# Where a delta layer's scan loads its decay row and makes its exponent arguments

## The reference, cut to what matters

```python
diff = gcum[..., :, None] - gcum[..., None, :]
decay_incl = jnp.where(incl, jnp.exp(jnp.where(incl, diff, 0.0)), 0.0)
a_mat = jnp.einsum('nbhid,nbhjd->nbhij', k_beta, kc) * decay_strict
t_mat = unit_lower_inverse(a_mat, cb)
...
def step(state, inp):
    q_i, k_i, w_i, u_i, qk_i, g_i = inp
    v_new = u_i - jnp.einsum('bhck,bhkv->bhcv', w_i, state)
    o_i = (jnp.einsum('bhck,bhkv->bhcv', q_i * jnp.exp(g_i)[..., None], state)
           + jnp.einsum('bhcj,bhjv->bhcv', qk_i, v_new))
    g_last = g_i[..., -1:]
    k_dec = k_i * jnp.exp(g_last - g_i)[..., None]
    state = state * jnp.exp(g_last)[..., None] + jnp.einsum('bhck,bhcv->bhkv', k_dec, v_new)
    return state, o_i
```

## Time and profile before

| what | value |
|---|---|
| median of three executions | 1416.29 us (1416.02 to 1417.29) |
| profiled execution, its own time | 1415.07 us |
| its span, first to last instruction | 1413.3 us |
| TensorE matmul busy | 1364.9 us, 97% of the span |
| VectorE busy | 822.2 us, 58% |
| ScalarE busy | 439.0 us, 31% |
| GpSimd busy | 269.5 us, 19% |
| mean granted TensorE clock | 0.999 of full speed |
| one head of the delta layer | 88.5 to 91.0 us |

### The profile page before, as it was taken

How to read it: one execution, slowest core, us unless ns; L and a number is a source line. 1 busy time by engine, 2 the same in 40 slices (tenths; PEclk the granted TensorE clock), 3 DMA queues, 4 the chain that set the end, 5 groups by cost and what they waited for, 6 DMA issues and landing times.

```text
span 1413.3 us, 30732 instructions
## 1 busy us (share of the span) xinstructions
PE 1364.9 (97%) x12976; PEld 929.3 (66%) x12976; DVE 822.2 (58%) x1834; ACT 439.0 (31%) x1062; POOL 269.5 (19%) x402
## 2 busy tenths in 40 slices
PE   5999999999999999999999999999999999989998
PEld 3577765666653445667777777778777778765543
DVE  4747772444432344775866858668486685862244
ACT  4114441444420322522323323233232331422211
POOL 1113200000000111431412314123141231310111
PEclk9999999999999999999999999999999999999999
DMA  9520108000055301201103022030120300430133
GB/s 367 227 48 32 38 0 326 1 1 1 3 226 226 129 30 60 59 32 34 62 3 95 34 56 73 3 94 35 30 98 3 95 34 6 164 136 25 47 119 119
DMA packets 56317, 112.16 MB, mean 79 GB/s; under 512 B 34698, under 2 KB 37586, under 8 KB 53346
## 3 DMA queue, kind: packets, MB, share of 16 engines
q1 hardware_dynamic: 56180, 110.21, 22.4%
HBM read 91.79 MB, written 18.40 MB: 78 GB/s over the span
## 4 chain that ended last, share of the span: by engine, by line
PE 65%; DVE 4%; issue 2%; ACT 0%; DVEq 0%; POOLq 0%; POOL 0%; ACTq 0%
PE psum L929 62%; PE psum L932 2%; DVE mem L2533 1%; DVE mem L2513 0%; DVE mem L2422 0%; DVE mem L2574 0%; DVE mem L2758 0%; DVE mem L2753 0%; DVE mem L2768 0%; DVE mem L2756 0%; DVE mem L2624 0%; DVE mem L2737 0%; DVE mem L2419 0%; DVE mem L2776 0%; DVE mem L2854 0%
## 5 line engine op out<-in xcount | busy, mean ns | idle before, releaser
L929 PE MATMUL psum<-mem 32*32 32x32 f32 (+11 forms) x12368 | 1304.1, 290 | 27.7 <-issue 10.0
L929 PEld LDWEIGHTS psum<-mem 32*32 32x32 f32 (+5 forms) x12368 | 860.4, 137 | 436.4 <-issue 231.1
L2533 DVE SCALAR_TENSOR_TENSOR mem<-mem 128x576 f32<-128x576 f32 (+1 forms) x126 | 112.3, 891 | 0.0
L932 PE MATMUL psum<-mem 128*128 128x128 f32 (+1 forms) x608 | 85.9, 278 | 15.0 <-ACT mem L1619 10.8
L932 PEld LDWEIGHTS psum<-mem 128*128 128x128 f32 (+1 forms) x608 | 71.3, 144 | 41.1 <-issue 25.7
L760 POOL TENSOR_SCALAR mem<-mem 128x1 f32<-128x1 f32 x17 | 3.6, 212 | 343.8 <-ACT mem L1762 343.8
L1926 ACT ACTIVATE mem<-mem 128x128 f32<-128x128 f32 x72 | 22.0, 305 | 135.3 <-DVE mem L2776 82.1
L2375 DVE SCALAR_TENSOR_TENSOR mem<-psum,mem 128x1024 f32<-128x1024 f32 x12 | 15.2, 1271 | 60.4 <-POOL mem L762 60.4
L1741 ACT ACTIVATE mem<-mem 128x256 f32<-128x256 f32 x72 | 35.5, 494 | 46.4 <-DVE mem L2335 46.4
L1762 ACT ACTIVATE mem<-psum 128x1024 f32<-128x1024 f32 x12 | 12.3, 1024 | 110.5 <-PE psum L929 108.7
L2075 DVE TENSOR_SCALAR mem<-psum,mem 128x128 f32<-128x128 f32 x64 | 21.1, 404 | 39.1 <-PE psum L932 39.1
(11 more groups left out here) (242 smaller groups left out, 1191.4 us busy)
## 6 DMA issues: line engine op xcount, KB each, us to landing
mem<-modw SPq DMA_DIRECT2D x12, 2048.0 KB, 13.3
mem<-w SPq DMA_DIRECT2D x44, 512.0 KB, 4.3
mem<-x SPq DMA_DIRECT2D x1, 4608.0 KB, 18.1
x_dram<-mem SPq DMA_DIRECT2D x9, 512.0 KB, 2.6
mem<-row_dram SPq DMA_DIRECT2D x8, 576.0 KB, 6.3
mem<-x_dram SPq DMA_DIRECT2D x9, 512.0 KB, 3.7
mem<-wout SPq DMA_DIRECT2D x4, 1024.0 KB, 8.6
mem<-gs SPq DMA_DIRECT2D x8, 512.0 KB, 3.3
```

The lines of the kernel that those rows point to most:

```text
L929: return pe.matmul(*a, **k)
L932: return pe.transpose(out, in_, ident[0:n, 0:n])
L2533: x = dve.scalar_tensor_tensor(cvm, U1[:, m, lo + j:hi + j], CW[:, 3 * g + ORDER[m], j:j + 1], cvm, ALU.mult, ALU.add)
```

## The change

Two edits. On SyncE's queue the decay row is issued ahead of the history and the weights, with its wait for the last product that still reads `EE`. On VectorE the first five arguments are made in step 1, none in step 2, two in step 3 and two in step 4; three each in steps 2, 3 and 4 were made before.

```diff
                 if ahead:
+                    sp.wait_ge(sem("eq_ready"), 3 * h + 3)
+                    rows(h + 1)
                     sp.wait_ge(sem("s1_ready"), 3 * h + 3)
                     history(h + 1)
                     if h:
...
                     weights(h + 1, 3)
-                    sp.wait_ge(sem("eq_ready"), 3 * h + 3)
-                    rows(h + 1)
                     if h:
                         sp.wait_ge(sem("y1_done"), 3 * h)
...
-                    if ahead and k in (2, 3, 4):
-                        exponents(h + 1, 3 * (k - 2), 3 * (k - 1))
+                    if ahead and k in (1, 3, 4):
+                        exponents(h + 1, *{1: (0, 5), 3: (5, 7), 4: (7, NT)}[k])
                     between(h, 14 + 3 * k, ahead)
```

## The result

The changed kernel takes 1408.47 us in the median (1406.05 to 1409.61, five executions) against 1416.02 us (1415.53 to 1417.29) for the kernel before on the same chip: a ratio of 0.9943, 95% interval 0.9931 to 0.9954, so 6.5 to 9.8 us faster. A second set of executions of it gave 0.9950 (0.9936 to 0.9963). Forecast was 1412.2 us, with a range from 1411.0. The direction was right; the gain is nearly twice the forecast and lies outside the range.

What follows compares the result with a forecast made beforehand. TensorE, busy 97% of the span, was taken as the bound, with 6.1 us of waits on VectorE to win. Terms -1.85 and -2.3 gave -4.1 us, median 1416.29 to 1412.2 us; range 1411.0 to 1419.0.

Steps and rivals of the forecast that it cites:

- Five arguments in step 1 cost nothing: VectorE, step 1: they take 1.35 us, and the 0.06 us delay is swallowed by 0.36 us of idleness.
- The row is there: SyncE's queue: the decay row lands 4.6 us after issue (bounds 3.9 to 5.8), needed by 4.7, up to 5.1 swallowed.
- The rival's own case: Row late: landing 5.8 us after issue puts `RR` of step 2 1.2 us late; 1419.8 us; chance 0.21.
- `RR` of step 3, first term, -1.85 us: TensorE's 0.36 us wait for `RR` vanishes once arguments leave step 2: 5 x 0.37 = -1.85 us.
- The bound of 6.1 us: All TensorE waits on `SP` and `RR`, 4.62 + 4 x 0.37 us, as the most the change can return.
- d, the shift of the sums, 1.7 us with 2.2 as upper bound: Weights, and so GpSimd's sums, come later behind the row: 1.7 us taken, bounds 0.5 and 2.2.
- What d does: Later sums miss VectorE's taps in step 2, so `SP` waits fall from 4.26 to 1.9 us: second term, -2.3 us.
- The rule for starts of 6.7 to 7.3 us: Sums starting then, counted from `RR` of step 1, make TensorE wait for `SP`: wait = start - 6.3.
- Two in place of three in steps 3 and 4: VectorE has 0.27 us less at each step; worth nothing, as the table shows no TensorE waits there.
- The sum: -1.85 - 2.3 = -4.1 us on the profiled execution: 1415.07 becomes 1411.0, the median 1416.29 becomes 1412.2 us.

Runs made afterwards that it cites:

- e6: Against the kernel before: arguments placed as in the change (five in step 1, two in step 3, two in step 4), queue as before; ratio 1.0297.
- e5: Against the kernel before: queue as before, no arguments in steps 1 and 2, two in step 3, four in step 4, three in step 5; ratio 0.9965.
- e4: Against the changed kernel: the history's three small loads issued behind the weights instead of ahead of them; ratio 0.9957 to the kernel before.
- e7: The change with weights ahead of the history, plus GpSimd's weight sums held until `SP` of step 2 is made; ratio 0.9948 to the kernel before.
- e2: Against the changed kernel: row still first, but three arguments each in steps 1, 3 and 4; ratio 0.9945 to the kernel before.
- e1: Against the kernel before: only the decay row issued first, arguments left three each in steps 2, 3 and 4; ratio 1.0044.

## Why the prediction was right in kind and wrong in size

- **Five arguments in step 1 cost nothing.** Right. They take 1.40 us with nothing ahead of them, and the addition behind `RR` still waits 0.35 us for TensorE.
- **The row is there.** Right: 4.1 us to landing where 4.6 was taken, and 4.7 needed. e6 shows a row that is late, by 4.6 us in head 1, and that little of it is swallowed: 6.1 us of delay. The rival's own case, 1.2 us late, was not run; its price left out that late arguments meet the sums and that the clock falls behind the wait.
- **`RR` of step 3, first term, -1.85 us.** The wait went in all five heads. Its size failed: e5, with the queue of before, gained 3.3 us between SP 2 and SP 3. The step that failed is "5 x 0.37 = -1.85 us": the matmul row's idle time was taken for the price of the wait, and the price is 0.63 us.
- **The bound of 6.1 us.** Wrong for the same reason, and this capped the whole forecast. In head 1 the `SP` wait was 0.41 us in the matmul row and `SP` of step 2 came 0.78 us earlier without it. In heads 1, 3, 4, 5 and 6 the gain is 0.37 or 0.38 us above the wait.
- **d, the shift of the sums, 1.7 us with 2.2 as upper bound.** Mis-sized. It is 2.35 to 3.5 us in the seven heads. The working counted the row's bytes and its one issue, and took the history's issues as fixed at 1.66 us; they took 3.4 us, up to 5.0 in head 4. So the weights are issued 2.1 to 2.6 us later, and 0.2 to 1.3 us more come between issue and the sums' start. The 1.7 us for the row's bytes fit e4, where the block behind the row takes 1.3 to 3.0 us longer to land; the issue behind it was the part left out. The bound was no upper bound.
- **What d does.** Right in its mechanism, as e4 and e7 show together. The rule for starts of 6.7 to 7.3 us (wait = start - 6.3) had only head 0 left to apply to in the change: it starts at 7.00, and its wait is 0.7. The rule had no case for the longest wait, 1.0 us in head 2: there the first sum and the first tap start together, 6.08 us after `RR`, and the tap takes 1.89 us in place of 0.81. In e5 head 6 has a start of 6.07 and the same wait of 1.0. In e4 head 4's sum starts at 7.61, past the mask product, and `SP` is 0.34 us off the floor of 10.52 in place of 1.3. In the other six heads of the change the starts lie above 8.5 us and TensorE's matmuls no longer wait at `SP` of step 2. Of the 4.26 us of waits 3.6 went, where 2.3 were forecast. By the mark this is 6.6 us: of the 4.3 us above the forecast, 1.3 come from more waits gone (the larger d) and 3.0 from the price of each.
- **Two in place of three in steps 3 and 4: "worth nothing".** Wrong for step 3: 1.65 us between SP 3 and SP 4 in seven heads. The table of matmul waits has no entry there, and the weight loads' row has: TensorE's weight load of step 4 waited for `RR` in each head.
- **The sum.** Scans: -1.85 - 2.3 were forecast, 8.5 us were measured, of which some 6.6 in step 2 (the sums' start), 0.3 net in step 3 (what `RR` gains, less what VectorE there now loses to the sums) and 1.65 in step 4. Of the 8.5 us, 6.2 reach the next head's start; 0.4 us come from ahead of the first scan; together 6.6, the span's difference.

What is open in part: the 2.35 us lost between step 7 and the next head's start. The granted clock accounts for some of it. In head 6 of the changed kernel TensorE has a gap of 2.7 us that the profile charges to nothing (1.4 us before), and right behind it come the 3.41 us at half clock shown above; from step 7 to the next head this head takes 54.04 us where it took 52.90. The second profile of the same kernel has half the clock for 6.83 us at this place and takes 55.97:

```profile
1239.12:1245.95 6.83, 6.12 (x71) 4.80 (x72) 1.45 (x3) 0.16 (x1) 0.00 (x0) 0.50 0.62 242
```

Over all profiles here this stretch takes 52.5 to 53.1 us with no such fall, 53.3 to 55.2 with one of 3.41 us, and 55.7 to 56.0 with one of 6.83. So 1.1 of the 2.35 us in the first profile, and 3.1 of the 3.4 in the second, lie in the one head where the clock falls, gap included. The rest is not explained: head 3 loses 1.4 us and head 5 0.8 at full clock, and the four others gain 0.9 together. In head 3 the same stretch takes 48.6 us in the second profile of the same kernel, and up to 51.1 in other runs, so that part is no steady cost of the change. TensorE's gaps charged to nothing change place from run to run, and their total is only 0.7 us more than before. All other variants show a loss of 2.1 to 4.4 us outside the scans too, except e4, which loses none and whose clock does not fall there; in e2 the clock does not fall either, and it loses 2.6 us, 2.3 of them in head 3. The kernel before has one profile here, and its own spread is not known.

That the two edits need each other was seen only from one side. The prediction said that a late row makes the arguments in step 1 dear. It did not say that the row's new place, with the arguments left in step 2, is a loss: e1 is 6 us slower, and its scans lose 1.8 us even without the clock's part.

## What to carry to other kernels

When two engines exclude each other instruction by instruction, as VectorE and GpSimd do in e1, a burst on one costs the other one whole instruction per instruction, so keep short instructions out of the burst's window and let long ones meet it. The price of a wait on TensorE is better read in its weight loads than in its matmuls: here 0.82 and 0.86 us for gains of 0.63 and 0.78, where the matmuls had 0.36 and 0.41. A load that is moved ahead in a queue slows what stands right behind it, in its landing or in its issue: count both. And where a variant makes TensorE wait for some microseconds, look at the granted clock before all of the loss is put down to the wait.

## What the runs showed of the hardware that was not expected

- Three small loads of 12 KB each (3184 of the 3698 packets between 749 and 763 us are under 512 bytes) took 1.66 us to issue with nothing ahead of them, and 3.4 to 5.0 us right behind a load of 576 KB. With two blocks of weights between (e4) it was 6.04 us in head 1, and 5.4 to 6.9 in heads 1 to 6.
- VectorE and GpSimd alternated strictly: in head 1 of e1 each of three 128x128 instructions waited for a different weight sum (0.91, 1.42, 1.42 us, where one takes 0.27 to 0.34 alone).
- The granted TensorE clock fell to half for 3.41 or 6.83 us at a time, near long waits of TensorE: in every scan of e6, where it waits 3.2 to 6.0 us for `RR`, and in two of the four heads of e1 in which it waits 1.9 to 2.5 us. In e6 the same work from `RR` to `SP` took 4.67 us in place of 4.20.
- The decay row, one row of `row_dram` read for 128 partitions, lands in 3.9 us at the least when nothing is ahead of it, the same as 512 KB of weights with only the history ahead.
